# Input sums from GpSimd to VectorE, and two copies ahead of the hidden product in ScalarE's order

## The reference, cut to what matters

```
def conv_ffn(xn, buf, w_up, w_conv, b_conv, w_down):
    u, gt = jnp.split(xn @ w_up, 2, axis=-1)          # D_MODEL 1024 -> 2 * D_FF, D_FF = 2816
    up = jnp.concatenate([buf.astype(u.dtype), u], axis=1)
    conv = b_conv
    for j in range(CONV_W):                           # CONV_W = 3
        conv = conv + w_conv[j] * up[:, j:j + t]
    y = (jax.nn.silu(conv) * gt) @ w_down
    return y, up[:, -(CONV_W - 1):]
```

## Time and profile before

| | us |
|---|---|
| median of 3 runs | 1778.86 (1774.74 to 1783.17) |
| the profiled execution | 1784.24 |
| its span in the profile | 1782.5 |

### The profile page before, as it was taken

How to read it: one execution, slowest core, us unless ns; L and a number is a source line. 1 busy time by engine, 2 the same in 40 slices (tenths; PEclk the granted TensorE clock), 3 DMA queues, 4 the chain that set the end, 5 groups by cost and what they waited for, 6 DMA issues and landing times.

```text
span 1782.5 us, 37507 instructions
## 1 busy us (share of the span) xinstructions
PE 1620.0 (91%) x14375; PEld 1453.3 (82%) x14375; DVE 1052.6 (59%) x2502; ACT 721.9 (40%) x1585; POOL 352.3 (20%) x450
## 2 busy tenths in 40 slices
PE   6999999979899989898989999998898989889897
PEld 5999865559898989888889997545798989889896
DVE  4434456656686665757564344575748775756755
ACT  3322256533334442635342213663433352533524
POOL 1001114412322211212001101342215121211101
PEclk9999999999999999999989999999999999999999
DMA  9335395475537765856133537625851584856631
GB/s 345 111 119 180 134 326 197 133 221 86 177 83 184 149 164 117 192 121 142 51 92 92 180 107 249 204 72 163 176 187 50 126 194 122 183 124 139 169 69 56
DMA packets 234898, 266.76 MB, mean 150 GB/s; under 512 B 16074, under 2 KB 176266, under 8 KB 234268
## 3 DMA queue, kind: packets, MB, share of 16 engines
q1 hardware_dynamic: 209088, 210.90, 38.6%
q0 software_dynamic: 25632, 53.47, 16.3%
HBM read 218.21 MB, written 16.68 MB: 132 GB/s over the span
## 4 chain that ended last, share of the span: by engine, by line
PE 49%; DMA 17%; DVE 9%; PEld 8%; issue 5%; ACT 4%; SPq 2%; DVEq 2%; POOL 1%; PEldq 1%; ACTq 0%; POOLq 0%
PE ps L1109 13%; DMA slab<-slab 8%; PEld ps L1719 8%; DMA slab<-in_w_up 7%; PE ps L1719 7%; PE ps L1539 6%; PE ps L952 2%; PE ps L1248 2%; PE ps L1233 2%; PE ps L1160 2%; PE ps L1093 1%; PE ps L1598 1%; PE ps L1571 1%; PE ps L1205 1%; PE ps L1104 1%
## 5 line engine op out<-in xcount | busy, mean ns | idle before, releaser
L3410 POOL DMA_DIRECT2D slab<-slab x144 | 124.3, 937 | 555.9 <-DMA slab<-in_w_up 387.8
L1109 PE MATMUL ps<-slab_r,work_r 128*128 128x256 f32 x960 | 205.6, 282 | 0.0
L1719 PE MATMUL ps<-side_r,big_r 128*128 128x272 f32 x696 | 147.8, 294 | 18.6 <-DVE big_r L2429 18.6
L1109 PEld LDWEIGHTS ps<-slab_r,work_r 128*128 128x128 f32 x960 | 157.8, 188 | 2.7 <-issue 2.5
L1598 PE MATMUL ps<-work_r,more_weights_r 128*128 128x272 f32 x432 | 111.4, 310 | 43.9 <-ACT xnT L2205 41.8
L1719 PE MATMUL ps<-side_r,slab_r 128*128 128x272 f32 x696 | 145.2, 290 | 0.0
L1719 PE MATMUL ps<-big_r 128*128 128x272 f32 x696 | 144.9, 290 | 0.0
L2218 ACT ACTIVATE big<-work,colsB 128x560 f32<-128x560 f32 x36 | 27.5, 765 | 253.0 <-DVEq L3114 253.0
L1719 PEld LDWEIGHTS ps<-side_r,big_r 128*128 128x128 f32 x696 | 109.9, 190 | 22.8 <-DVE big_r L2429 21.3
L1598 PEld LDWEIGHTS ps<-work_r,more_weights_r 128*128 128x128 f32 x432 | 79.4, 201 | 50.5 <-ACT xnT L2205 46.8
L1719 PEld LDWEIGHTS ps<-big_r 128*128 128x128 f32 x696 | 110.6, 191 | 0.0
(11 more groups left out here) (553 smaller groups left out, 4596.7 us busy)
## 6 DMA issues: line engine op xcount, KB each, us to landing
slab<-in_w_up SPq DMA_DIRECT2D x180, 256.0 KB, 4.6
slab<-in_w_mod SPq DMA_DIRECT2D x22, 2048.0 KB, 10.6
slab<-slab POOLq DMA_DIRECT2D x144, 256.0 KB, 4.7
slab<-in_w_in SPq DMA_DIRECT2D x20, 1024.0 KB, 5.8
slab<-in_w_down SPq DMA_DIRECT2D x20, 1024.0 KB, 7.2
slab<-in_cache_cmp_kv SPq DMA_DIRECT2D x128, 128.0 KB, 2.0
slab<-in_cache_sel_kv SPq DMA_DIRECT2D x96, 128.0 KB, 2.0
big<-in_cache_win_kv SPq DMA_DIRECT2D x16, 512.0 KB, 7.6
```

Of the source, the lines that this page charges most:

```text
L1109: ins = mm(ps[n % 4][:, 0:cw], x, fr(wt[:, k, :]), start=k == 0 and m == 0, stop=k == KC - 1 and m == 2)
L1719: ins = mm(ps[bank + b][:, 0:HALF], wt, fr(x[:, k, HALF * b:HALF * b + HALF]), start=k == 0 and n == 0, stop=k == n_k - 1 and n == 2)
L3410: pool.dma_start(block_of(kind, c), src, accum_op=ALU.add).then_inc(sums_in[kind], 16)
```

## The change

Two things. The input sums are no longer on GpSimd but on VectorE, where `input_sum(2q)` and `input_sum(2q + 1)` close the work of each of the first four blocks (q = 0 to 3). And in rounds 5 to 21, ScalarE does `product5_out(c)`, the high part of M4(c) and `sum6_out(c)` directly after the high part of M3(c), ahead of `split_h(c - 1)` and of the first `split_down`.

```
@@ -2269,14 +2269,14 @@
                     if more_up:
                         high("M2", c + 1)
                     high("M3", c)
+                    product5_out(c)
+                    high("M4", c)
+                    sum6_out(c)
                     split_h((c - 1) % 4, c - 1)
                     if g < NG and q in (1, 2):
                         if q == 1:
                             act.wait_ge(slab_in[1], slab_loads("ffn", 1, L, g))
                         split_down(2 * q - 2, 1)
-                    product5_out(c)
-                    high("M4", c)
-                    sum6_out(c)
                     if more_up:
                         high("M5", c + 1)
                     else:
@@ -3175,6 +3175,20 @@
                     if g == NG and L + 1 < DEPTH and 2 <= c < 6:
                         low_first(c - 2, L + 1)
 
+                def input_sum(i):
+
+                    if i == 0:
+                        dve.wait_ge(x_lo.sem, x_lo.at(x_n2(KC - 1, 1), L))
+                        dve.wait_ge(cv_t.sem, cv_t.at(1, L))
+                    drain()
+                    if i < 4:
+                        dst, ks, ts = ((T1, K1, t1), (T3, K1, t2), (T2, K2, t2), (T4, K2, t1))[i]
+                        tt(dst, fr(hiX[:, ks, ts]).bitcast(F), fr(xnT[:, ks, ts]).bitcast(F), ALU.add)
+                    else:
+                        dst, x, y, how = ((T1, T1, T3, ALU.subtract), (T3, T2, T3, ALU.subtract), (T2, T2, T1, ALU.add),
+                                          (T4, T2, T4, ALU.subtract))[i - 4]
+                        tt(dst, x, y, how).then_inc(t_sum.sem, 1)
+
                 for q in range(CL):
                     conv(q % 2, q)
                     if q == 3:
@@ -3187,6 +3201,8 @@
                         low_block("M1", CL)
                     for k in ((), (0, 1), (2, 3), ())[q]:
                         split_down(k, 1, 0)
+                    input_sum(2 * q)
+                    input_sum(2 * q + 1)
                 low_input_sum(0)
                 low_input_sum(1)
                 u_first(CL)
@@ -3390,21 +3406,6 @@
-                def input_sums():
-
-                    pool.wait_ge(x_lo.sem, x_lo.at(x_n2(KC - 1, 1), L))
-                    pool.wait_ge(cv_t.sem, cv_t.at(1, L))
-                    for dst, ks, ts in ((T1, K1, t1), (T3, K1, t2), (T2, K2, t2), (T4, K2, t1)):
-                        G(dst, fr(hiX[:, ks, ts]).bitcast(F), fr(xnT[:, ks, ts]).bitcast(F), ALU.add)
-                    pool.drain()
-                    G(T1, T1, T3, ALU.subtract).then_inc(t_sum.sem, 1)
...
@@ -3435,7 +3436,6 @@
                         pool.wait_ge(*sum_at("M3", c - 1, L))
                     added("M3", c, block_of("M6", c))
 
-                input_sums()
                 third_sum(CL)
                 first_sum(CL)
                 for c in range(CL, FC):
```

More of the change, by code:

```diff
@@ L3392, in _ @@
                     put(by_part(s_win[L][b][0:WINDOW - NT]), by_part(A["cache_win_kv"][L][b][NT:WINDOW]))
-                def input_sums():
-                    pool.wait_ge(x_lo.sem, x_lo.at(x_n2(KC - 1, 1), L))
-                    pool.wait_ge(cv_t.sem, cv_t.at(1, L))
-                    for dst, ks, ts in ((T1, K1, t1), (T3, K1, t2), (T2, K2, t2), (T4, K2, t1)):
-                        G(dst, fr(hiX[:, ks, ts]).bitcast(F), fr(xnT[:, ks, ts]).bitcast(F), ALU.add)
-                    pool.drain()
-                    G(T1, T1, T3, ALU.subtract).then_inc(t_sum.sem, 1)
-                    pool.drain()
-                    G(T3, T2, T3, ALU.subtract).then_inc(t_sum.sem, 1)
-                    pool.drain()
-                    G(T2, T2, T1, ALU.add).then_inc(t_sum.sem, 1)
-                    pool.drain()
-                    G(T4, T2, T4, ALU.subtract).then_inc(t_sum.sem, 1)
                 def added(kind, c, src):
```

## The result

The changed kernel takes 1790.40 us (median of 7 runs, 1783.20 to 1796.21), the kernel before 1773.84 us (7 runs, 1771.57 to 1783.17). The ratio is 1.0083, 95% interval 1.0055 to 1.0111: 0.8% slower, some 15 us. The forecast was 1778 us, no change that can be measured, with a range up to 1790: the time lies just outside it. Counted from the forecast's own starting point of 1778.86 us, that upper bound is a loss of 11 us, and the measured loss is 15. The profiled execution of after took 1783.20 us, the fastest of its seven, and that of before 1784.24 us, above all seven of its own.

The account below looks back on a forecast made before the run. In the convolution-FFN stage it singled out TensorE's waits for an early hidden product (12.1 us) and product five's copy (41.8 us). 1784.24 - 7.0 + 6.0 = 1783.2 us profiled; with the median 5.4 us lower, 1778 us, range 1763 to 1790.

Parts of the forecast that it names:

- Part one: Input sums moved from GpSimd to VectorE ahead of each layer's first down-projection: -7.0 us, bounds -11.5 and -2 us.
- the stretch: VectorE instructions in layer 0, lengthened while GpSimd makes the input sums: 14.1 us expected to go.
- the wait inside: TensorE's wait for the first residual at the first down-projection's third column: 2.2 us.
- Rival C: VectorE is simply full and GpSimd did not cause its long instructions: +20 us, 1799 us, chance 0.04.
- Part two: ScalarE's new order in 17 rounds of each layer: +6.0 us, bounds 0 and +12 us.
- (a): Down-projection rounds: where the transfer releases ScalarE, the moved group delays the down-projection by 1.08 us; 1.6 us over eight.
- rival B: Hidden part now depends on product six, late when TensorE leaves product four's wait at half clock: 1790 us, chance 0.14.
- (b): Round right after a down-projection: ScalarE waits for product six, 0.4 us in each of four rounds without cover; +1.6 us.
- (c): Last round of each layer: down weights' high parts queue behind the copy of sum six, 0.85 us each, 1.7 us.
- (d): Fewer, longer TensorE waits, clock mostly halved from about 2.5 us: +1.5 us at down-projections, +0.7 us in the first group.
- (e): Eight rounds with two down-weight parts: the second starts about 0.1 us earlier, -1.1 us in all.
- A: ScalarE, not the transfer, decides, so product three's earlier start pays off: 1762 us, even towards 1730; chance 0.22.

Follow-up runs that it names:

- e14: Second run of the input sums alone: sums on VectorE, ScalarE's order as in the kernel before; 1773.10 us, ratio 0.9978.
- e1: The changed kernel with ScalarE's order as in the kernel before, so only the input sums moved to VectorE; 1774.25 us, ratio 0.998.
- e8: Input sums on VectorE, ScalarE's new order only in the eight rounds with a down-projection, old order elsewhere; 1781.49 us, ratio 1.0027.
- e5: The changed kernel with ScalarE's new order only in first and second rounds after a down-projection and each layer's last round; 1774.81 us, ratio 0.9987.
- e0: The changed kernel run once more, unaltered, for a second profile; 1789.96 us, ratio 1.0071.
- e2: The kernel before with only ScalarE's order changed, input sums still on GpSimd; 1793.58 us, ratio 1.0093.
- e6: The changed kernel with ScalarE's new order only in third rounds after a down-projection and rounds with one; 1784.66 us, ratio 1.0033.
- e9: Input sums on VectorE, ScalarE's old order, hidden product's high part made twice in the eight down-projection rounds; 1785.85 us, ratio 1.0054.
- e15: Against the kernel before: input sums on VectorE, low parts of the first two behind the first residual, ScalarE's old order; 1765.96 us, ratio 0.9934.

## Why the prediction was wrong, by its own steps

**Part one, -7.0 us: right.** The up parts are 3.5 and 3.4 us shorter, 6.9 us in all (5.3 us in e14, where layer 1 gained 1.6 us only). Each term is there: the stretch goes, the sums take 1.33 us with their drains (2.67 us the pair; 1.35 taken), and the wait inside is 2.03 us (2.2 taken). The whole program gained less by the medians, 3.5 and 3.9 us. One interval reaches from 8 us less to 1 us more, the other from 8 us less to no change, so by time alone the gain isn't clear of noise, and whether some of it is paid back later stays open. By the rule cited with it, that a saturated VectorE should be relieved, the change would have made the kernel slower; e1 and e14 say that it did not. The Trainium skill, SBUF — State Buffer, section SBUF: two separate sides, says that a VectorE instruction with two SBUF inputs and a GpSimd one that reads SBUF hold a shared pair of ports by turns, each for its whole length, and that the other then blocks. The trace agrees in kind: the two-input instructions of 0.80 us took 2.9 us. Rival C is out.

**Part two, +6.0 us: it was +15 in the rounds and +2.4 at the end of layer 1.** The place where the loss would come was right, its cost was not. By its terms:

- (a) Down-projection rounds, forecast 1.6 us: the waits ahead of the eight down-projections grew from 12.1 to 16.8 us, 4.7 us. The step counted the group only where the transfer releases ScalarE, and held that elsewhere its 1.15 us of idle time cover it. Round 16 of layer 1 shows otherwise. ScalarE in time in after, then in e1, there with TensorE's first row of the down-projection:

```profile
1622.02 0.40 ACT L2212 ACTIVATE rstd<-ps 128x272 f32<-128x272 f32 x1
1622.31 0.65 ACT L2168 ACTIVATE side_r<-big 128x544 fp32r<-128x544 f32 x1
```

```profile
1615.47 0.66 ACT L2168 ACTIVATE side_r<-big 128x544 fp32r<-128x544 f32 x1 [1.04 <-DVE big L3131]
...
1616.94 0.39 PE L1719 MATMUL ps<-side_r,big_r 128*128 128x272 f32 x1 [1.11 <-DVE big_r L2429]
```

 Product six ends at 1621.98 in after; the copy of its sum follows at 1622.02, then the hidden part, and the down-projection starts 1.79 us behind product six. In e1 the hidden part starts 0.36 us before product six ends (1615.83), and the down-projection 1.11 us behind it. Seven of the 24 down-projections under the new order waited exactly 1.79 us, and none waited less; under the old order waits went down to 1.06 us, but for one of 0.40. That floor is rival B's dependence, though at another place than B said. Of these 0.68 us only 0.2 us are the group standing ahead; for 0.5 us the hidden product itself is late (it ends 0.1 us behind product six, in e1 0.4 us before it). Over all down-projections of these nine profiles the two share the 4.7 us evenly: the hidden part starts 0.39 us behind the hidden product's end in place of 0.09, which is 2.4 us for eight, and the hidden product ends 0.24 us behind product six in place of 0.05 ahead of it, 2.3 us. The forecast had something near the first and nothing for the second. I read the second as TensorE, with less of a wait at product three, being further ahead of VectorE; in e8, where the other rounds keep the old order, it is absent (0.04 us ahead). That is argued from one profile.
- (b) The round right after a down-projection, forecast +1.6 us: it became 12.6 us shorter instead, and the third rounds 12.9 us longer. The forecast's picture held in that waits move and the three kinds together take as long as before (323.9 us in place of 323.3), and e5 shows it: new order in the first rounds moves the loss into third rounds that have the old one. What holds the sum is open. The forecast took the transfers; but in the third rounds of after ScalarE waits for one 0.09 us on average, and VectorE, whose busy time fell from 10.0 to 7.7 us in a first round, is busy 11.7 of 14.3 us in a third one (e1: 9.4 of 12.5). VectorE's own queue is a rival that no run tests.
- (c) The last round, forecast 0.85 us per layer: right. TensorE waits 1.66 us ahead of the last down weights in after, 0.82 us in the second profile of before:

```profile
1744.09 0.39 PE L1707 MATMUL ps<-side_r,big_r 128*128 128x272 f32 x1 [1.66 <-DVE slab_r L2429]
```

```profile
1739.74 0.39 PE L1707 MATMUL ps<-side_r,big_r 128*128 128x272 f32 x1 [0.82 <-DVE slab_r L2429]
```

 But in the stage table the part behind the last cut is 40.6 us in all four profiles with the new order in the last round of layer 1 (after, e0, e2, e5). With the old one there it is 38.2 us in seven profiles and 39.8 us in three. The 2.4 us are the 0.84 us of that wait and a step of 1.6 us, and this step is the clock again: some 10 us behind the last cut it falls to half in each of the seven profiles at 39.8 and 40.6 us, and in none of those at 38.2. In after it shows here (columns as the earlier trace rows):

```profile
1751.20:1753.20 2.00, 2.00 (x12) 1.76 (x10) 1.17 (x5) 1.24 (x2) 0.66 (x1) 0.51 0.00 0
```

- (d) The clock, forecast +2.2 us in all: this is the step that failed. The eight down-projections took 203.3 us in place of 193.3: +10.0 us, since in 22 of 24 the clock fell to half near the start, where it did in 4 of 48 before. The forecast put 1.5 us there: it looked for clock losses behind waits of 2.5 us and more; here waits of 1.79 us did it. Together (a) and (d) are 14.7 us of the 15.0 us that the rounds grew. The trace of before had one such case already, in round eight of layer 1 (TensorE in time, and then the columns of the earlier trace rows):

```profile
1474.32 0.52 PE L1719 MATMUL ps<-side_r,big_r 128*128 128x272 f32 x2 [1.79 <-DVE big_r L2429]
...
1475.23:1478.64 3.41, 3.41 (x17) 3.41 (x17) 0.61 (x1) 0.00 (x0) 0.86 (x1) 0.50 1.05 228
```

 Outside these down-projections the stretches at half clock grew shorter, 20.7 us under the new order and 29.6 us under the old (rounds 5 to 21, mean of three and of six profiles), and yet the rounds without a down-projection took no less in sum. So in this kernel the half clock costs its full 1.5 us inside a down-projection, and nothing that shows in the sum elsewhere.
- (e) The earlier down-weight part, forecast -1.1 us: not seen in any sum of rounds.

**The rivals.** A (the earlier product three pays off) came half: product three did start earlier and the first rounds are shorter, but third rounds pay it back. B came out at the right time, 1790 us, by luck: its +11 us stood on a start that was 5 us too high. It named the dependence on product six; its mechanism, ten slow rounds behind product four, is not what happened, the third rounds' loss being only time moved there from the first ones. Its condition, a wait at product four above 2.7 us in most rounds, was not met either: 33.6 us in 16 waits are 2.1 us each.

**The starting point.** The forecast subtracted 5.4 us for the profiled execution as a whole and let its rounds stand. They were 2.9 and 4.8 us longer than those of the next two profiles. It touches no step, but the long stage of that profile hid in the first comparison of the traces (-1.1 us) what the medians showed.

**What stays open:** which of TensorE's waits decide that the clock is halved, and what paces the other rounds. Under the old order 15 down-projections waited 1.75 us or longer, and the clock fell in four of them; under the new order all 24 waited as long, and it fell in 22. e6 and e8 don't settle what differs: both keep the old order in the round two places ahead, e6 with the new one in the round just ahead had seven of eight, e8 without it five of eight, three of them behind waits of exactly 1.79 us, and two more waits of 1.79 us left the clock full.

## What to carry to other kernels

Moving a copy out of TensorE's way gains nothing where something else sets how long several rounds take together: the wait turns up at another product. Before putting work ahead of an instruction that releases a long run of matmuls, count what it costs there twice, once as the delay and once as the clock, which can fall early in the run; here the second was two thirds. And take more than one profile of each kernel when the difference is under 1%, and cut them at fixed instructions, so that the untouched part drops out.

## What the runs showed of the hardware

- The granted clock can fall behind short waits: in round 16 of layer 1 of after, 1.79 us of idle time ahead of a down-projection, at a granted clock of 1.00, and then 0.68 over its first 3.2 us. It cost some 1.5 us (25.5 against 24.03 us). It doesn't fall each time: in 11 of 15 waits of 1.75 us and more under the old order it stayed full.
- A wait that grows by 0.9 us at such a place therefore costs 1.7 us (e9: 13.8 us for eight of them).
- Eight 128x1088 additions in each layer are cheaper on VectorE itself, at 1.29 us each, than on GpSimd, where they stretched VectorE's own instructions (0.80 us became 2.9 us): the up parts are 6.9 us shorter over the two layers.
- The fastest kernel found, e15 (input sums on VectorE, low parts of the first two sums behind the first residual, ScalarE's old order), takes 1765.96 us, ratio 0.9934 (0.9912 to 0.9956).
